# Five joints of a two-model block kernel: two weight blocks instead of one start on the unnormed x, with masks and reciprocal deviation in PSUM and one block's low halves on GpSimd

## The chip, the cores and the metric

The kernel runs on one core of a Trainium2 chip. The metric is the time of one execution on the device, in microseconds; the kernel before was timed three times, and the median counts. TensorE is called PE in the rows, VectorE DVE, ScalarE ACT, GpSimd POOL and SyncE SP.

## The reference, cut to what matters

Two models follow each other on one sequence of 256 tokens with 1024 features, all in float32. The first block is an adaptive RMS norm, a wide projection, a 31-tap convolution branch, a Mamba-2 scan, two output projections and a gated MLP. The second has a gated delta rule layer and a gated linear attention layer, each with an MLP of 4096 hidden features. What the change touches are the five places where a norm stands between two big matrix products:

```python
h = rms_norm(x, norm_ffn_w[i]) * (1.0 + scale) + shift          # joint "ffn"
x = x + gate * ffn_sublayer(h, w_ffn_in[i], w_ffn_down[i])
return rms_norm(x, final_norm_w)                                # joint "final"
...
m = _mixer_gdn(x, a_w_in[j], ...)        # qkv = silu(conv(x @ a_w_in)), decays exp(cumsum(g))
x = _layernorm(ALPHA * x + m, ln1_g[i], ln1_b[i])               # joints "ln1_0", "ln1_1"
x = _layernorm(ALPHA * x + relu(x @ w1) ** 2 @ w2, ln2_g[i], ln2_b[i])   # joint "ln2_0"
```

## The kernel before, in words

**Products.** x is kept feature-major: 8 tiles of 128 features by 256 tokens. A weight matrix comes in blocks of 1024 rows by 256 columns (1 MB), through a ring `raw` of four slots that SyncE fills in order. A block is two tiles (h = 0, 1) of 128 output features. To reach float32 accuracy each operand is split in a rounded high half and the rest: ScalarE copies `raw` to `whi` (L463, `split_hi`), VectorE or GpSimd subtracts to get `wlo` (L473, `split_lo`), both in rings of four tiles, that is, two blocks. TensorE then runs whi·HH + whi·HL + wlo·HH over 8 tiles of x (L596 to L598), 24 matmuls for a tile and 48 for a block, into one of four PSUM banks `acc`. A slot of `raw` is released by `split_lo`.

**Sections.** `split_section` walks a matrix on ScalarE, VectorE or GpSimd, `pe_section` on TensorE: after the splits for block b+1 come the results of block b, then `extra(b)`. Every engine works through its list in the order in which the program writes it; semaphores tie the lists together. The order is written by hand, there is no scheduler.

**Joints.** A norm needs all 8 tiles of the new x, which the last section before it (w_out, ffn_down, a_out, mlp2_0, b_out) produces two at a time with VectorE (L1957, L1961). So that TensorE isn't idle meanwhile, block 0 of the section behind a norm (ffn_in, a_qkv, mlp1_0, b_qk, mlp1_1) takes x unnormed: `act_first` makes squares SQX (L760) and the high half of gain times x, GHI (L761); `low_halves` makes GLO on VectorE (L794); `pe_early` multiplies block 0 with them, in between sums squares and x over features with matmuls against ones (L697 to L707: float32 operands, two records for each), and `scale_first` on VectorE repairs the product afterwards with mean and reciprocal deviation (L857 to L864). `norm_dve` meanwhile centres x (L934), scales it (L940), and makes the low half HL (L956) of the normed x; ScalarE makes the high half HH (L909). Block 1 (`pe_first`, L530 to L537) already needs HH, and HL right behind. `norm_pool` (L965, L967) writes the normed x back to X for the residual. Blocks 0 and 1 of the early section share their whi/wlo rings and PSUM banks with what is before them.

**a_qkv.** Each of its 12 blocks needs 8 operations of VectorE for a five-tap convolution (L1814) behind a copy by ScalarE (L1413); in blocks 3 to 10 VectorE also makes the decay matrices: six products of a 128x128 mask and a column (L2017 to L2021, `decay_sides`). The low halves of the weights are GpSimd's here. Behind the section TensorE reads the decay matrices (L2492).

ffn_in also carries four loads of 1 MB of adaptive-norm weights (`ADA_PLAN`) in the same ring `raw`, used up by VectorE (L1671).

## Time and profile before

| | us |
|---|---|
| median of 3 runs | 1563.12 (1562.01 to 1563.95) |
| the profiled execution | 1563.59 |
| its span, first to last instruction | 1561.9 |
| PE busy | 1428.2 (91%), 10981 matmul records |
| DVE busy | 1012.4 (65%) |
| ACT busy | 774.1 (50%) |
| POOL busy | 396.3 (25%) |
| chain that ended last, PE's share | 73% |
| chain that ended last, DVE's share | 13% |

Matmuls overlap, so a record lasts 284 ns while the next starts long before; what counts on TensorE is the distance from start to start. The joints lie at 452 us (ffn), 657 us (final), 963 us (ln1_0), 1162 us (ln2_0) and 1345 us (ln1_1).

### The profile page before, as it was taken

To read this page: it belongs to the slowest core of one execution; us is meant where nothing else is said; L and a number is where in the kernel's file an instruction comes from. 1 tells how busy PE (TensorE), PEld (TensorE's weight loads), DVE (VectorE), ACT (ScalarE), POOL (GpSimd) and SP (SyncE) were. 2 spreads that over 40 slices of the span, in tenths; PEclk is the share of its full clock that TensorE was granted. 3 is DMA by queue.
4 is the path that set the end of the run, shared out by engine and by line. 5 is a ranking of instruction groups with operands and counts; after the bars stand their busy time and mean duration, and the time that the engine had idled before them with its cause. 6 is when DMAs were issued, how large, how long until landed. Compare 5 with 4: busy or idle time off the path is not lost.

```text
span 1561.9 us, 27505 instructions
## 1 busy us (share of the span) xinstructions
PE 1428.2 (91%) x10981; PEld 1374.3 (88%) x10981; DVE 1012.4 (65%) x1739; ACT 774.1 (50%) x1211; POOL 396.3 (25%) x340
## 2 busy tenths in 40 slices
PE   4989999989898999898988889999999987999998
PEld 4989998988898999898878879999997976899997
DVE  5687868557676665669655557874465565876443
ACT  3434466574363433464573445664354634666333
POOL 1555774304300000157372400730005000200000
PEclk9899999999899999989999999999999999999999
DMA  9954553233746745625310005455553510365540
GB/s 355 365 163 133 165 162 109 82 108 121 238 155 218 226 157 162 208 81 162 109 55 1 1 1 162 139 186 181 178 167 97 178 39 10 127 189 184 174 155 28
DMA packets 202480, 223.74 MB, mean 143 GB/s; under 512 B 7608, under 2 KB 197723, under 8 KB 200317
## 3 DMA queue, kind: packets, MB, share of 16 engines
q1 hardware_dynamic: 201072, 220.67, 43.8%
q8 instruction: 80, 1.31, 0.4%
q10 hardware_dynamic: 1293, 1.47, 0.3%
q14 instruction: 35, 0.29, 0.1%
HBM read 221.07 MB, written 1.05 MB: 142 GB/s over the span
## 4 chain that ended last, share of the span: by engine, by line
PE 73%; DVE 13%; ACT 6%; issue 3%; DMA 2%; POOL 2%; SPq 0%; DVEq 0%; ACTq 0%; POOLq 0%
PE acc L596 18%; PE acc L598 17%; PE acc L597 17%; DVE GB L1814 2%; POOL H L967 1%; PE acc L530 1%; ACT whi L463 1%; PE acc L537 1%; DVE wlo L473 1%; PE acc L531 1%; DMA raw<-in_w_ffn_in 1%; DMA XIN<-in_x 1%; DVE SQX L940 1%; POOL AM L1185 1%; PE pm L2346 1%
## 5 line engine op out<-in xcount | busy, mean ns | idle before, releaser
L596 PE MATMUL acc<-HH,whi 128*128 128x256 f32 x1744 | 500.2, 287 | 26.3 <-issue 10.6
L463 ACT ACTIVATE whi<-raw 128x1024 fp32r<-128x1024 f32 (+2 forms) x380 | 378.8, 1029 | 241.3 <-PE acc L598 194.1
L597 PE MATMUL acc<-HL,whi 128*128 128x256 f32 x1744 | 495.1, 284 | 0.0
L598 PE MATMUL acc<-HH,wlo 128*128 128x256 f32 x1744 | 494.7, 284 | 0.0
L473 DVE TENSOR_TENSOR wlo<-raw,whi 128x1024 fp32r<-128x1024 f32 (+2 forms) x292 | 339.3, 1194 | 206.3 <-ACT whi L463 203.7
L596 PEld LDWEIGHTS acc<-HH,whi 128*128 128x128 f32 x1744 | 333.1, 191 | 34.0 <-issue 22.2
L597 PEld LDWEIGHTS acc<-HL,whi 128*128 128x128 f32 x1744 | 332.9, 191 | 0.3 <-issue 0.2
L598 PEld LDWEIGHTS acc<-HH,wlo 128*128 128x128 f32 x1744 | 332.8, 191 | 0.0
L473 POOL TENSOR_TENSOR wlo<-raw,whi 128x1024 fp32r<-128x1024 f32 x88 | 217.8, 2494 | 426.7 <-DVE wlo L473 272.1
L596 PE MATMUL acc<-HIDH,whi 128*128 128x256 f32 x688 | 195.7, 284 | 6.4 <-ACT whi L463 4.5
L598 PE MATMUL acc<-HIDH,wlo 128*128 128x256 f32 x688 | 195.4, 284 | 0.0
L597 PE MATMUL acc<-HIDL,whi 128*128 128x256 f32 x688 | 195.4, 284 | 0.0
L596 PEld LDWEIGHTS acc<-HIDH,whi 128*128 128x128 f32 x688 | 132.8, 193 | 7.0 <-issue 7.0
L597 PEld LDWEIGHTS acc<-HIDL,whi 128*128 128x128 f32 x688 | 132.8, 193 | 0.0
L598 PEld LDWEIGHTS acc<-HIDH,wlo 128*128 128x128 f32 x688 | 132.8, 193 | 0.0
L1800 DVE SCALAR_TENSOR_TENSOR pm<-UP,par,pm 128x256 f32<-128x256 f32 x158 | 66.9, 482 | 0.0
L530 PE MATMUL acc<-HH,whi 128*128 128x256 f32 x128 | 42.4, 351 | 15.6 <-ACT HH L909 6.7
L1552 ACT ACTIVATE TMP<-acc 128x256 f32<-128x256 f32 x60 | 23.1, 385 | 63.7 <-PE acc L598 58.9
L1185 POOL TENSOR_TENSOR AM<-ATT,gm 128x512 f32<-128x512 f32 x28 | 38.4, 1395 | 59.1 <-DVE ATT L2101 41.8
L2182 DVE TENSOR_TENSOR TMQ<-TMP 128x256 f32<-128x256 f32 x64 | 28.9, 452 | 37.4 <-ACT HIDH L1555 37.4
L1814 DVE SCALAR_TENSOR_TENSOR GB<-acc,par,GB 128x254 f32<-128x254 f32 (+1 forms) x96 | 45.1, 480 | 9.2 <-ACT GB L1413 6.4
L967 POOL TENSOR_SCALAR X<-SQX,par 128x256 f32<-128x256 f32 x8 | 8.2, 1036 | 159.4 <-DVE SQX L940 159.4
(542 smaller groups left out, 2531.1 us busy)
## 6 DMA issues: line engine op xcount, KB each, us to landing
raw<-in_mlp_w SPq DMA_DIRECT2D x64, 1024.0 KB, 5.3
raw<-in_w_in SPq DMA_DIRECT2D x36, 1024.0 KB, 5.3
raw<-in_w_ffn_in SPq DMA_DIRECT2D x22, 1024.0 KB, 5.3
raw<-in_a_w_in SPq DMA_DIRECT2D x16, 1024.0 KB, 5.7
raw<-in_b_w_in SPq DMA_DIRECT2D x12, 1024.0 KB, 5.3
raw<-in_w_ada_mix SPq DMA_DIRECT2D x8, 1024.0 KB, 5.6
ADR<-in_w_ada_ffn SPq DMA_DIRECT2D x8, 1024.0 KB, 11.1
...
```

The lines of the kernel that those rows point to most:

```text
L463: act.activation(whi[:, (s.t0 + 2 * u + h) % 4, 0:k], raw[:, place(s, b, u) % 4, 0:k, h * P:h * P + P], ACT.Copy).then_inc(hi_ready, 1)
L473: v.tensor_tensor(wlo[:, slot, 0:k], raw[:, place(s, b, u) % 4, 0:k, h * P:h * P + P], whi[:, slot, 0:k].bitcast(F32), ALU.subtract).then_ ...
L530: pe.matmul(acc[:, q, 0:T], whi[:, slot, i], hh, start=i == 0, stop=False)
L596: pe.matmul(acc[:, q, 0:T], whi[:, slot, i], hh, start=first and i == 0, stop=False)
L597: pe.matmul(acc[:, q, 0:T], whi[:, slot, i], hl, start=False, stop=False)
L598: m = pe.matmul(acc[:, q, 0:T], wlo[:, slot, i], hh, start=False, stop=final and i == k - 1)
L967: pool.tensor_scalar(dst[:, k], SQ[name][:, k], shift(k) if shift else 0.0, None, ALU.add)\
L1185: pool.tensor_tensor(AM[u][:, lv % 2].rearrange("p (s c) -> p s c", s=4), ATT[u][:], mask, ALU.mult).then_inc(am_ok, 1)
L1552: act.activation(TMP[:, q], acc[:, out_slot(s, u, h), 0:T], ACT.Relu, bias=evac_bias(s, b, u, h))\
L1800: c.tick(v.scalar_tensor_tensor(ACC[:, i] if w_ == CW - 1 else sum_, src, wt, sums.get(i, sum_), ALU.mult, ALU.add))
L1814: ins = v.scalar_tensor_tensor(d_, x_, pc(w, i + 24 * tap), d_, ALU.mult, ALU.add)
L2182: c.link(v.tensor_tensor(TMQ[:, q], TMP[:, q], TMP[:, q], ALU.mult))
```

## The change

It does seven things.

1. In the five early sections blocks 0 and 1 both take x unnormed (`pe_early` with four tiles; `scale_first` is called for block 0 ahead of HL and for block 1 behind it). Block 2 is the first that takes HH and HL.
2. The order inside the joint is new: one sum of squares and one of x, added up on VectorE, go to TensorE ahead of the last tile of the section before (`pe_parts`); the splits of block 1 are slipped between the steps (`mid`, `norm_dve`, `early_act`); the table load of ScalarE is moved ahead.
3. The reciprocal deviation is written to PSUM (`pm[:, 1, T:]`) for the scaling of x, and to NR for `scale_first`.
4. The low halves of block 2 go to GpSimd (`third`), and `norm_pool` of these joints waits until HL is complete. GpSimd starts with a_qkv's block 3 only then too; blocks 0 and 1 are VectorE's.
5. ffn_down and mlp2_0 are unrolled, and consecutive column pairs take turns in the four PSUM banks.
6. The decay masks are copied to PSUM once (`masks_in_psum`), and `decay_sides` reads them there; TensorE waits for `gm_l` too.
7. The four adaptive-norm loads of ffn_in come behind blocks 3, 5, 7, 9 instead of 1, 3, 5, 7; shifts and the gate logits of ln2_0 come one block later.

```diff
-                "ffn_in": (0, 1, 0, 1, 0, 1, 0, 1) + (0,) * 14}
+                "ffn_in": (0, 0, 0, 1, 0, 1, 0, 1, 0, 1) + (0,) * 12}
...
-            return (s.o0 + h) % 4
+            return (s.o0 + h + (2 * j if s.flat else 0)) % 4
...
+                    if s.name in NORM_BEFORE and last and h == 1:
+                        pe_parts(pe, NORM_BEFORE[s.name])
...
+        def pe_parts(pe, name):
+            mean = NORM[name][1]
+            pe.wait_ge(part_ok, PARTS[name] + (2 if mean else 1))
+            if mean:
+                pe.matmul(pm[:, 0, 0:T], ones, NR[:, 0] if is_long(name) else XP[:, 0], start=True, stop=False)
+            pe.matmul(pm[:, 1, 0:T], ones, SQX[:, 0], start=True, stop=False)
...
+            with_lo(first, range(6))
+            with_hi(first, whi, (6, 7))
+            with_hi(first, wlo, (6, 7))
+            with_lo(first, (6, 7)).then_inc(w_used, 1)
+            for tile in tiles[1:]:
+                open_(tile)
+                with_hi(tile, whi, range(8))
+                with_lo(tile, range(7))
+                pe.wait_ge(raw_used, 2 * s.w0 + tile[0] + 1)
+                with_hi(tile, wlo, range(8))
+                with_lo(tile, (7,)).then_inc(w_used, 1)
...
+                act.activation(pm[:, 1, T:], NR[:, 1], ACT.Exp, scale=-0.5).then_inc(n_std, 1)
+                act.activation(NR[:, 1], NR[:, 1], ACT.Exp, scale=-0.5)
                 for h in range(2):
-                    split_hi(act, SEC[EARLY[name]], 1, 1, h)
+                    split_hi(act, SEC[EARLY[name]], 2, 2, h)
...
-                v.scalar_tensor_tensor(sq[:, k], src[:, k], scale(k), NR[:, 1], ALU.mult, ALU.mult).then_inc(n_t, 1)
+                v.scalar_tensor_tensor(sq[:, k], src[:, k], scale(k), pm[:, 1, T:] if e else NR[:, 1], ALU.mult, ALU.mult)\
+                 .then_inc(n_t, 1)
...
+            if name in EARLY:
+                pool.wait_ge(n_hl, 8 * HN[name] + 8)
...
+            def third(name):
+                s = SEC[EARLY[name]]
+                pool.wait_ge(raw_used, 2 * (s.w0 + 2))
+                for h in range(2):
+                    split_lo(pool, s, 2, 2, h)
...
+            third("ffn")
+            third("final")
+            pool.wait_ge(n_hl, 8 * HN["final"] + 8)
...
-                    v.tensor_scalar(LF[:, 2 * h + tk], slo[:, 0:P], gcol(gd, 0, tk, h), None, ALU.mult)
+                    v.tensor_scalar(LF[:, 2 * h + tk], s_lo, gcol(gd, 0, tk, h), None, ALU.mult)
...
+            def masks_in_psum():
+                for i, m in enumerate((slo[:, 0:P], suo[:, 0:P], maskb[:, P:2 * P], maskf[:, 0:P])):
+                    c.tick(v.tensor_copy(pm[:, 3, i * P:i * P + P], m))
+                c.wait()
```

VectorE's list at the joint ln1_1, from the last two tiles of x on, before (L473 is a low half of weights, X<-X,acc the residual, L857 to L864 `scale_first`):

```order
L1957 TENSOR_TENSOR X<-X,acc 128x256 x2
L794 SCALAR_TENSOR_TENSOR GLO_ln_0_105<-X,par,GHI_ln_0_104 128x256 x4
L473 TENSOR_TENSOR wlo<-raw,whi 128x1024 x2
L928 TENSOR_SCALAR NR<-pm 128x256
L929 SCALAR_TENSOR_TENSOR NR<-pm,NR 128x256
L931 SCALAR_TENSOR_TENSOR NR<-pm,NR 128x256
L934 SCALAR_TENSOR_TENSOR X<-pm,X 128x256 x8
L940 SCALAR_TENSOR_TENSOR SQX<-X,par,NR 128x256 x8
```

And in the changed kernel, from the last tile of x to the repair of block 1:

```order
L2047 TENSOR_TENSOR X<-X,acc 128x256
L474 TENSOR_TENSOR wlo<-raw,whi 128x1024
L823 SCALAR_TENSOR_TENSOR GLO_ln_0_105<-X,par,GHI_ln_0_104 128x256
L990 TENSOR_SCALAR NR<-pm 128x256
L991 SCALAR_TENSOR_TENSOR NR<-pm,NR 128x256
L474 TENSOR_TENSOR wlo<-raw,whi 128x1024
L994 SCALAR_TENSOR_TENSOR NR<-pm,NR 128x256
L996 SCALAR_TENSOR_TENSOR X<-pm,X 128x256 x8
L1002 SCALAR_TENSOR_TENSOR SQX<-X,par,pm 128x256 x8
L902 COPY WB<-acc 128x2 x2
L1022 SCALAR_TENSOR_TENSOR HL<-SQX,par,HH 128x256 x8
```

The low half of block 1's second tile now stands between the mean and the variance, the scaling reads PSUM, and the repair (rows L902 to L916) stands once ahead of HL and once behind it. Two rows of the repair between L902 and L1022 are the ones of L857 to L864, for both tiles at once.

TensorE's list at the same joint in the changed kernel, from the first early matmul on (GHI and GLO are the halves of gain times x):

```order
L704 MATMUL acc<-GHI_ln_0_104,whi 128x258 x6
L724 MATMUL pm<-X,maskf 128x256 x2
L704 MATMUL acc<-GHI_ln_0_104,wlo 128x258 x6
L730 MATMUL pm<-SQX,maskf 128x256
L733 MATMUL pm<-SQX,maskf 128x256 x2
L711 MATMUL acc<-GLO_ln_0_105,whi 128x258 x6
```

Five sums against ones stand here where there were ten; two more stand ahead of the last tile of b_out, and the low half's six products now follow within the first tile.

VectorE's list in a_qkv, the decay sides of one head, before and in the changed kernel:

```order
L2017 TENSOR_SCALAR LF<-slo,gd 128x128
L2018 TENSOR_SCALAR LB<-suo,gd 128x128
L2017 TENSOR_SCALAR LF<-slo,gd 128x128
L2018 TENSOR_SCALAR LB<-suo,gd 128x128
L2020 TENSOR_SCALAR GM<-maskb,gd 128x128
L2021 TENSOR_SCALAR GM<-maskf,gd 128x128
```

```order
L2123 TENSOR_SCALAR LF<-pm,gd 128x128
L2124 TENSOR_SCALAR LB<-pm,gd 128x128
L2123 TENSOR_SCALAR LF<-pm,gd 128x128
L2124 TENSOR_SCALAR LB<-pm,gd 128x128
L2126 TENSOR_SCALAR GM<-pm,gd 128x128
L2127 TENSOR_SCALAR GM<-pm,gd 128x128
```

Nothing is moved here; the six operations read their mask from PSUM.

## Rows read from the trace of the kernel before

**Rows 1.** Windows: stretch; its us, busy time of PE, PEld, DVE, ACT, POOL; PEclk; DMA.

```profile
451.60:466.60 15.00, 14.98 (x108) 13.86 (x107) 12.97 (x29) 13.35 (x23) 0.00 (x0) 1.00 0.43 141
656.80:677.70 20.90, 16.04 (x102) 15.04 (x103) 16.40 (x32) 11.94 (x22) 8.16 (x4) 0.84 0.39 113
963.10:984.00 20.90, 19.33 (x118) 16.26 (x117) 18.66 (x44) 13.56 (x25) 4.96 (x8) 1.00 0.31 101
1161.90:1183.00 21.10, 18.21 (x110) 16.05 (x109) 18.16 (x42) 11.50 (x20) 9.48 (x20) 0.92 0.31 99
1345.10:1367.80 22.70, 19.44 (x118) 16.20 (x116) 20.44 (x46) 14.84 (x27) 8.16 (x8) 1.00 0.30 94
530.00:590.00 60.00, 60.00 (x507) 60.00 (x507) 35.93 (x55) 24.35 (x31) 0.00 (x0) 1.00 0.49 157
```

**Rows 2.** Timeline of PE at joint ln1_1: start us, us, what [idle before <-releaser].

```profile
1345.83 1.46 PE L697 MATMUL pm<-SQX,maskf 128*128 128x256 f32 x6
1347.13 1.46 PE L700 MATMUL pm<-XP,maskf 128*128 128x256 f32 x6
...
1367.84 0.36 PE L596 MATMUL acc<-HH,whi 128*128 128x256 f32 x1 [1.44 <-issue]
```

**Rows 3.** Groups of DVE in 1345 to 1368: xcount | busy us, mean ns.

```profile
L473 DVE TENSOR_TENSOR wlo<-raw,whi 128x1024 fp32r<-128x1024 f32 x4 | 4.7, 1221 | 1.8 <-ACT whi L463 1.8
L956 DVE SCALAR_TENSOR_TENSOR HL<-SQX,par,HH 128x256 fp32r<-128x256 f32 x8 | 3.9, 554 | 0.0
L940 DVE SCALAR_TENSOR_TENSOR SQX<-X,par,NR 128x256 f32<-128x256 f32 x8 | 3.8, 548 | 0.0
L934 DVE SCALAR_TENSOR_TENSOR X<-pm,X 128x256 f32<-128x256 f32 x8 | 2.7, 414 | 0.0
L859 DVE SCALAR_TENSOR_TENSOR acc<-NR,WB,acc 128x256 f32<-128x256 f32 x2 | 1.0, 490 | 0.1
...
L2182 DVE TENSOR_TENSOR TMQ<-TMP 128x256 f32<-128x256 f32 x2 | 0.8, 416 | 0.0
```

**Rows 4.** Waits of PE in 640 to 760: us in total, times, longest.

```profile
PE acc L596 <- DVE GB L1814: 5.3, 2, 3.7
PE acc L692 <- DVE X L1961: 4.9, 1, 4.9
PE pm L2492 <- DVE LB L2018: 2.1, 1, 2.1
PE acc L596 <- issue: 1.9, 2, 1.7
```

**Rows 5.** Windows at the joint final, columns as in rows 1.

```profile
661.00:668.00 7.00, 6.34 (x28) 5.83 (x29) 2.64 (x6) 5.59 (x9) 2.50 (x2) 0.58 0.25 89
...
681.00:688.00 7.00, 7.00 (x36) 7.00 (x37) 3.03 (x7) 1.08 (x2) 4.71 (x3) 0.55 0.66 166
```

**Rows 6.** Timeline of DVE before the joint final and in a_qkv.

```profile
652.50 6.73 DVE L794 SCALAR_TENSOR_TENSOR GLO_final<-X,par,GHI_final 128x256 fp32r<-128x256 f32 x6
...
721.11 0.28 DVE L2018 TENSOR_SCALAR LB<-suo,gd 128x128 f32<-128x128 f32 x1
...
723.84 2.39 DVE L2020 TENSOR_SCALAR GM<-maskb,gd 128x128 f32<-128x128 f32 x1
...
731.41 3.97 DVE L1814 SCALAR_TENSOR_TENSOR GB<-acc,par,GB 128x254 f32<-128x254 f32 x8
```

**Rows 7.** Timeline of POOL in a_qkv.

```profile
721.41 4.73 POOL L473 TENSOR_TENSOR wlo<-raw,whi 128x1024 fp32r<-128x1024 f32 x2 [0.32 <-ACT whi L463]
```

**Rows 8.** Timeline of DVE: the same kind of operation with its input in PSUM.

```profile
918.89 0.34 DVE L2137 TENSOR_SCALAR VNA<-acc,ab__690 128x128 f32<-128x128 f32 x1
919.15 0.34 DVE L2136 TENSOR_SCALAR VNA<-acc,ab__690 128x128 f32<-128x128 f32 x1
```

**Rows 9.** Waits of PE in 440 to 530, around the start of ffn_in.

```profile
PE acc L596 <- issue: 5.0, 4, 1.4
PE acc L596 <- ACT whi L463: 1.9, 3, 0.7
```

More of the change, by code:

```diff
@@ L488, in body @@
                 for h in range(2):
-                    if s.name in NORM_OF and eng is not nc.gpsimd and b == 0:
+                    if s.name in NORM_OF and b in (0, 2):
                         continue
-                    if split and not last:
+                    if split and s.name in NORM_OF and b == 1:
+                        if split is split_lo and h == 0:
+                            eng.wait_ge(raw_used, 2 * (s.w0 + 3))
+                        split(eng, s, 3, 3, h)
+                    elif split and not last:
                         split(eng, s, b + 1, u + 1, h)
@@ L497, in body @@
                         evac(b, u, h, j)
+                        if mid and last and h == 0:
+                            mid()
                 if extra:
@@ L633, in program @@
         XC0 = {"conv": 0, "ln1_0": 8, "ln2_0": 17, "ln1_1": 26, "ln2_1": 35}
-        PARTS = {"ffn": 0, "final": 1, "ln1_0": 2, "ln2_0": 4, "ln1_1": 6}
+        PARTS = {"ffn": 0, "final": 2, "ln1_0": 3, "ln2_0": 6, "ln1_1": 8}
         RANK = {name: i for i, name in enumerate(EARLY)}
@@ L681, in pe_early, with with_hi, with_lo, open_ @@
             o0 = SEC[BEFORE[name]].o0 + 4
-            place_ = [(h, (s.t0 + h) % 4, out_slot(s, 0, h)) for h in range(2)]
-            for h in range(2):
-                pe.wait_ge(hi_ready, s.t0 + h + 1)
-                pe.wait_ge(raw_used, 2 * s.w0 + h + 1)
-            late = 2 if SEC[BEFORE[name]].chunks > 1 else 0
-            pe.wait_ge(acc_free, s.o0 + late + 1)
-            def with_hi(h, slot, q, ks):
+            tiles = [(2 * b + h, (s.t0 + 2 * b + h) % 4, out_slot(s, b, h)) for b in range(2) for h in range(2)]
+            def with_hi(tile, weights, ks):
+                i, slot, q = tile
                 for k in ks:
                     pe.wait_ge(g_hi, g + k + 1)
-                    pe.matmul(acc[:, q, 0:w], whi[:, slot, k], hi[:, k, 0:w], start=k == 0, stop=False)
-            with_hi(*place_[0], range(6))
-            px, ps = parts(name)
-            pe.wait_ge(part_ok, PARTS[name] + (2 if mean else 1))
-            for i, t_ in enumerate(ps):
-                pe.matmul(pm[:, 1, 0:T], ones, t_, start=i == 0, stop=False)
+                    pe.matmul(acc[:, q, 0:w], weights[:, slot, k], hi[:, k, 0:w],
+                              start=k == 0 and weights is whi, stop=False)
+            def with_lo(tile, ks):
+                i, slot, q = tile
+                for k in ks:
+                    pe.wait_ge(g_lo, g + k + 1)
+                    m = pe.matmul(acc[:, q, 0:w], whi[:, slot, k], lo[:, k, 0:w], start=False, stop=k == 7)
+                return m
+            def open_(tile):
+                i = tile[0]
+                pe.wait_ge(hi_ready, s.t0 + i + 1)
+                pe.wait_ge(acc_free, s.o0 + i + 1)
+            first = tiles[0]
+            open_(first)
+            with_hi(first, whi, range(6))
             if mean:
-                for i, t_ in enumerate(px):
-                    pe.matmul(pm[:, 0, 0:T], ones, t_, start=i == 0, stop=False)
                 for k in (6, 7):
@@ L704, in pe_early @@
                 m.then_inc(n_mean, 1)
+            pe.wait_ge(raw_used, 2 * s.w0 + 1)
+            with_hi(first, wlo, range(6))
+            if not is_long(name):
+                pe.wait_ge(part_ok, PARTS[name] + (3 if mean else 2))
+                pe.matmul(pm[:, 1, 0:T], ones, SQX[:, 4], start=False, stop=False)
             for k in (6, 7):
@@ new lines, in more, with mid @@
+                if b == last - 1 and name in ("ffn", "final"):
+                    v.wait_ge(raw_used, 2 * e.w0)
+                    for h in range(2):
+                        split_lo(v, e, 0, 0, h)
+            def mid():
+                if not is_long(name):
+                    v.wait_ge(n_sq, 8 * n + 6)
+                    v.tensor_tensor(SQX[:, 4], SQX[:, 4], SQX[:, 5], ALU.add).then_inc(part_ok, 1)
+                low_halves(v, c, name, (6,))
+            return dict(extra=more, mid=mid)
@@ L1169, in _ @@
             pool.nop().then_inc(mask2, 1)
-            lo_section(SEC["a_qkv"])
+            third("ffn")
+            third("final")
+            pool.wait_ge(n_hl, 8 * HN["final"] + 8)
+            s = SEC["a_qkv"]
+            for b in range(3, s.nb):
+                for h in range(2):
+                    split_lo(pool, s, b, b % 4, h)
+            for h in range(2):
+                split_lo(pool, SEC["a_z"], 0, 0, h)
             lo_section(SEC["a_z"])
@@ L1186, in _ @@
                                            ALU.mult).then_inc(am_ok, 1)
+            third("ln1_0")
             norm_pool(pool, "ln1_0", par_col("ln1_b"), X)
@@ L1206, in _ @@
                     sums_to(W05[:, lv // 2, d, lv % 2 * P:lv % 2 * P + P], lv, d)
+            third("ln2_0")
             pool.wait_ge(n_t, 8 * NORM["ln2_0"][0] + 1)
@@ L1219, in _ @@
             pool_shift(pool, "ln2_0")
+            third("ln1_1")
             norm_pool(pool, "ln1_1", par_col("ln1_b", 8), X)
```

282 lines of the change are left out of this document (158 added, 124 removed).

## The prediction

> **What bounds the kernel now.** The first view to read is the chain that ended last: TensorE has 73% of it, VectorE 13%. So the question is where TensorE isn't fed. The second is a quiet stretch: between 530 and 590 us TensorE starts 507 matmuls in 60 us, at a granted clock of 1.00 [rows 1]. With a few records missing I use 0.119 us from start to start, so a block of 48 costs 5.71 us. A sum against ones costs more: three of them (six records) fill the 1.30 us from 1345.83 to 1347.13 [rows 2], 0.43 us each. With these two prices every joint can be billed. A joint's own work is 96 matmuls, 11.4 us, and its sums [all rows 1]:
>
> - ffn: 15.0 us, own 11.4 + 5 x 0.43 = 13.6, lost 1.4.
> - final: 20.9 us, own 11.4 + 3 x 0.43 = 12.7, lost 8.2; the 4.9 us wait for VectorE's X [rows 4] is in it.
> - ln1_0: 20.9 us, own 11.4 + 10 x 0.43 = 15.7, lost 5.2; ln1_1 likewise 22.7 - 15.7 = 7.0.
> - ln2_0: 21.1 us, own 11.4 + 6 x 0.43 = 14.0, lost 7.1.
>
> The joints lose 29 us. A third view, the waits of TensorE in a_qkv, adds 5.3 + 2.1 + 1.9 = 9.3 us [rows 4]. In ffn_in another 6.9 us go in seven waits, three of them for ScalarE's high half, that is, for weights that came late [rows 9].
>
> **What sets the wait in a joint.** VectorE's list. At ln1_1 it is busy 20.4 of 22.7 us [rows 1], and block 2 starts only at 1367.84, 1.44 us after TensorE was through with block 1 [rows 2]; VectorE's low half of block 2 is the last thing it needs. With two blocks early, TensorE has 5.7 us more to do before it asks for HH, and that covers the waits for HH and HL. What is late next must be asked of VectorE's list again, since block 3's low half stands behind everything.
>
> **ln1_1 and ln1_0.** TensorE first. The two sums moved ahead of the last tile are only moved, but they wait for VectorE: behind the sixth tile of x come a square and GHI on ScalarE, then a GLO and four additions, some 4.1 us at 0.42 to 0.49 each, against TensorE's tile of 2.9 us. So 1.2 us are waited there, and with the sums themselves (0.9) the first early matmul comes 2.1 us later than now. Then 96 matmuls and five sums, 13.6 us, and block 2, 5.7: TensorE could start block 3 at 21.4 us behind today's first early matmul, or at 23.3 in ln1_0, with its shift of 16 matmuls in between. Now VectorE, whose last tile of x is there 0.95 us behind the first early matmul: low half 1.2, GLO 0.5, mean 0.86, low half 1.2, variance 0.43, centring 2.7, scaling 2.7 (from PSUM: I take L934's price, the same form with one input in PSUM, not L940's 3.8), repair 2.1 (2 x (0.15 + 0.49 + 0.43)), HL 3.4 (8 x 0.42, L2182's price for two inputs in SBUF, since GpSimd's X now waits; L956's 3.9 beside GpSimd is the other end), repair 2.1, TMQ and HIDL of block 0 1.7, low half of block 3 1.2 [rows 3]. That is 20.1; with 2.1 and 0.95 it ends at 23.2, and 0.9 later because GpSimd's X runs beside its last part. So block 3 starts at 24.1. Today it starts at 22.7 + 5.7 = 28.4 (ln1_0: 28.5, with its shift). Gain 4.3 each; block 4's low half then comes 0.3 late: **4.0 each, 8.0 together**. GpSimd's two low halves of block 2, 2.4 us each [rows 7], start when ScalarE has split it and end some 3 us ahead of TensorE's need. Bounds: 2 each if VectorE's last part pays double for two-input operations, 5.2 if the parts aren't waited for.
>
> **ln2_0.** The same list, but the sums are ready long before, and VectorE is through with block 3's low half at 21.8 us, ahead of TensorE, which does shift and gate logits first. New is a wait: the logits need all of X, which GpSimd writes only behind HL now. HL is done at 17.5 us, eight operations at ln1_0's 0.62 us (4.96 for 8, rows 1) take 5.0, and TensorE asks at 0.9 + 13.1 + 5.7 + 1.9 = 21.6: 0.9 late. Behind GpSimd's X stand its masks W67 and the shift of X, which nobody needs before b_v is done. **7.1 - 0.9 = 6.2 us**; bounds 3 (ln1_1's 1.02 us each, rows 1) and 7.1.
>
> **ffn.** One sum less, 0.4. Block 2 waits 0.5 for ScalarE (table load and gate of block 0 stand behind HH), the parts 0.3, hops and HL 0.5: 1.3 lost instead of 1.4, and the first of the seven waits, 1.0 us before block 3, is covered. **1.5 us**, bounds 0 and 2.5. The four adaptive-norm loads sit in the same ring two blocks later with the same pattern (a slot is freed by VectorE behind block b, reloaded, and split for block b+3). I count the other 5.9 us [rows 9] as moved, not saved; bounds -1 and +3.
>
> **final and a_qkv.** (1) VectorE was late with X because six GLO took 6.7 us while GpSimd split a_qkv's block 0 [rows 6]; alone they would take 6 x 0.42 = 2.5. GpSimd is silent there now, and the banks take turns, so the wait of 4.9 goes, but for 0.6 for the last square. (2) Behind that wait the granted clock was 0.58 over 7 us [rows 5], that is, 1.2 GHz for most of them; without the wait I take it as 2.4 GHz. With the rest of the loss, (1) and (2) give 8.2 - 0.6 = 7.6. (3) The waits in a_qkv. A mask product takes VectorE 0.28 us alone, but 2.4 when GpSimd is in a low half, and it ends (723.84 + 2.39) when GpSimd's pair ends (721.41 + 4.73) [rows 6, 7]. The convolution, with an input in PSUM, keeps its 3.97 us for eight. With the masks in PSUM each product takes 0.26 from start to start [rows 8], six 1.6: VectorE's need for a block becomes 3.9 + 1.6 = 5.5 us, just below TensorE's 5.71. TensorE keeps 1.4 before block 4 (ScalarE's exponential behind VectorE's gates, then ScalarE's and GpSimd's halves) and 0.9 before block 5: 9.3 - 2.3 = 7.0. Together **14.6 us**. The second low stretch, 0.55 at 681 to 688 [rows 5], began behind small products of 32 columns, and these stay: its 3.2 us (0.45 x 7) stay. The four copies of masks cost 1.0 by the PSUM price, 2.4 more if one meets a GpSimd operation; VectorE is 3 us ahead of block 5 there. The added wait on `gm_l` costs two mask products, 0.5, behind b = 10, ahead of block 11's end.
>
> The rows say that a mask in SBUF waits for GpSimd and an input in PSUM doesn't. The Trainium skill's page "SBUF — State Buffer", section "Who interferes with whom", states a lock behind it: outside the two-port modes an operation of VectorE with at most one SBUF input doesn't contend. The same section speaks against `third`: an operation with two SBUF inputs contends with a GpSimd operation that reads SBUF. By it HL and the additions beside `third` would wait, which is rival B.
>
> **The rivals.** (B) VectorE's list is longer than billed: `third` and GpSimd's X slow its two-input operations as at 652 us (1.12 each instead of 0.42) [rows 6]. Then the ln1 joints and ffn give nothing: 1532.8 + 9.5 = 1542. For it: busy 20.4 of 22.7 us. Against: `third` lies beside centring and scaling, which have an input in PSUM. (C) PSUM doesn't free VectorE, the change doesn't do what it says: the GB and LB waits stay (7.0), and each of four joints pays a GpSimd low half of 2.4: 1532.8 + 16.6 = 1549. Against: the 3.97. (D) The parts are there in time (3 x 1.2) and the clock doesn't fall at 681 (3.2): 1526. (E) Slower: the clock falls in the early stretch of the joints, as it did behind the wait of 4.9. TensorE waits 1.2 us for the parts, and again for squares; if each joint then runs its 96 early matmuls at 1.2 GHz, that costs 11.4 us each, 57 in all: 1590. It decides from three joints on. Against: ln1_1's window shows 1.00 despite a wait of 1.44 [rows 1, 2].
>
> **How the numbers follow.** 1.5 + 14.6 + 8.0 + 6.2 = 30.3. The profiled execution took 1563.6 (span 1561.9 and 1.7 around it), 0.5 above the median: 1563.6 - 30.3 = 1533.3, against the median 1532.8. Chances: this case (1528 to 1537) 0.55, B 0.20, D 0.14, C 0.08, E 0.03. The range 1522 to 1545 takes in B and D with their bounds and leaves out C and E. A difference under 0.2% (3 us) can't be told from none: faster 0.95, same 0.02, slower 0.03.
>
> **What would show it.** Scaling of x at 2.7 us for eight; mask products all at 0.26 from start to start; no wait of TensorE for GB over 1 us in a_qkv behind block 5; the first block with HH starting without a wait; block 3 of mlp1 waiting for VectorE's low half; no low clock around 661. Wrong would be: waits for the parts over 2 us, GpSimd's low half as releaser of block 2, a granted clock under 0.9 in a joint, or more than 7 us of waits in ffn_in.

## The result, and the profile after

The changed kernel took 1519.61 us (median of 4 runs, 1518.09 to 1522.63) against 1562.57 for the kernel before: ratio 0.974, 95% interval 0.972 to 0.976. That is 43 us faster, where 30.3 were forecast, and 2.4 us below the range. Run once more beside the kernel before it took 1521.69 (6 runs, 1517.78 to 1528.29), ratio 0.977 (0.974 to 0.980), so 36 to 43 us is what the change gives. The profiled execution of the first set is its slowest, 1522.63, with a span of 1520.9 against 1561.9: 41.0 us between the two traces, and these are accounted for below. A wait is given as the rows print it, as TensorE's idle time, or, where starts are compared, from start to start less the 0.12 us that a matmul takes anyway, which is some 0.16 us more.

The windows from a joint's first early matmul to its last [before: rows 1], in the order ffn, final, ln1_0, ln2_0, ln1_1 (us, busy of PE, PEld, DVE, ACT, POOL, PEclk, DMA):

```profile
451.60:465.40 13.80, 13.27 (x104) 12.55 (x102) 11.95 (x27) 10.83 (x21) 4.82 (x2) 1.00 0.58 182
653.90:666.60 12.70, 12.54 (x102) 12.09 (x101) 9.00 (x19) 9.77 (x21) 4.80 (x2) 1.00 0.67 176
940.90:954.60 13.70, 13.70 (x108) 13.44 (x107) 13.53 (x34) 9.43 (x20) 4.77 (x2) 1.00 0.52 162
1131.30:1146.40 15.10, 13.49 (x107) 13.07 (x105) 14.56 (x36) 8.79 (x19) 5.96 (x4) 1.00 0.41 125
1308.70:1322.30 13.60, 13.60 (x108) 13.34 (x107) 13.43 (x34) 9.37 (x20) 4.77 (x2) 1.00 0.53 160
```

At both ln1 joints TensorE is busy all the time, and the clock is 1.00 in all five. TensorE's timeline at ln1_1 [before: rows 2] and at ln2_0 shows what is left: a wait for the part of x, none ahead of the first block with HH (1322.36), one ahead of block 3, and in ln2_0 one ahead of the first block with HH:

```profile
1304.88 0.70 PE L691 MATMUL pm<-XP,maskf 128*128 128x256 f32 x2 [1.07 <-DVE SQX L882]
...
1322.36 0.28 PE L537 MATMUL acc<-HH,whi 128*128 128x256 f32 x1
...
1329.31 0.35 PE L606 MATMUL acc<-HH,whi 128*128 128x256 f32 x1 [1.08 <-issue]
```

```profile
1146.47 0.36 PE L537 MATMUL acc<-HH,whi 128*128 128x256 f32 x1 [1.68 <-ACT QK L1660]
```

What ScalarE does ahead of that QK (the copy of block 0 out of its bank), with the repair's last operation on the bank's first tile by VectorE and the zeroing of the gate weights' tile `gw` by GpSimd:

```profile
1143.07 0.94 POOL L1295 MEMSET gw<- 33x1024 f32 x1
1143.40 0.49 DVE L914 TENSOR_SCALAR acc<-acc,WB 128x256 f32<-128x256 f32 x1
1144.46 0.32 ACTq L1655 DMA_DIRECT2D gw<-in_b_gate_w  x1
...
1145.48 0.30 ACTq L1656 DMA_DIRECT2D gw<-in_b_gate_b  x1
1145.83 0.66 ACT L1660 ACTIVATE QK<-acc 128x256 f32<-128x256 f32 x2 [2.48 <-issue]
```

VectorE's groups in 1308 to 1331 [before: rows 3] (xcount | busy us, mean ns):

```profile
L474 DVE TENSOR_TENSOR wlo<-raw,whi 128x1024 fp32r<-128x1024 f32 x4 | 4.8, 1216 | 0.0
L1022 DVE SCALAR_TENSOR_TENSOR HL<-SQX,par,HH 128x256 fp32r<-128x256 f32 x8 | 3.2, 480 | 0.0
L1002 DVE SCALAR_TENSOR_TENSOR SQX<-X,par,pm 128x256 f32<-128x256 f32 x8 | 3.2, 476 | 0.0
L996 DVE SCALAR_TENSOR_TENSOR X<-pm,X 128x256 f32<-128x256 f32 x8 | 2.7, 415 | 0.0
```

TensorE's waits in 632 to 740, the joint final and a_qkv [before: rows 4]:

```profile
PE acc L606 <- issue: 1.4, 2, 1.0
PE pm L733 <- ACT SQX L786: 0.2, 1, 0.2
```

The mask products, with their input in PSUM, take 0.26 us from start to start in a_qkv too, under GpSimd's low halves [before: rows 6]:

```profile
693.33 0.34 DVE L2124 TENSOR_SCALAR LB<-pm,gd 128x128 f32<-128x128 f32 x1
693.59 0.34 DVE L2126 TENSOR_SCALAR GM<-pm,gd 128x128 f32<-128x128 f32 x1
693.85 0.34 DVE L2127 TENSOR_SCALAR GM<-pm,gd 128x128 f32<-128x128 f32 x1
```

**Where the 41.0 us went.** Like instructions of both traces are set side by side: the difference of their starts grows or shrinks where time is won or lost. The clock's part is (1 - granted clock) summed over windows of 1 us; it comes in pieces of 1.7 us.

| stretch | forecast | found | of it clock |
|---|---|---|---|
| up to the joint ffn | 0 | 0.8 | |
| ffn, ffn_in, start of ffn_down | 1.5 | 2.3 | 0 |
| final and a_qkv | 14.6 (2.9 of it clock) | 21.3 | 8.5 |
| ln1_0 | 4.0 | 5.1 | 0 |
| start of mlp2_0 | 0 | 1.9 | 1.7 |
| ln2_0 | 6.2 | 5.6 | 0 |
| gated linear attention | 0 | 1.5 | 1.7 |
| ln1_1 | 4.0 | 5.5 | 0 |
| start of mlp2_1 | 0 | -1.5 | -1.7 |
| last norm | 0 | -1.4 | -1.7 |
| sum | 30.3 | 41.1 | 8.5 |

Some 32.6 us are shorter waits, where 27.4 were forecast, and 8.5 are clock, where 2.9 were: of the miss of 10.8, 5.6 are clock and 5.2 are waits, these spread over many places with no more than 1.5 in one. (The rows are rounded; the traces differ by 41.0.) The kernel before also paid it behind each of VectorE's waits in a_qkv, at 728, 755 and 772, three stretches that the prediction didn't bill (before; in front of the third stands a wait of 1.2 us, at 771.8, which all kernels here have):

```profile
728.30:732.30 4.00, 3.78 (x20) 3.81 (x21) 3.86 (x13) 1.89 (x3) 0.14 (x1) 0.57 0.67 225
755.00:759.00 4.00, 3.99 (x21) 3.99 (x22) 3.79 (x10) 0.00 (x0) 0.00 (x0) 0.58 0.80 260
772.50:776.50 4.00, 4.00 (x6) 1.52 (x5) 0.00 (x0) 1.37 (x3) 0.00 (x0) 0.57 0.73 237
```

The same work in the changed kernel, 17 to 24 us earlier (from 711, 734 and 749 us), runs at 1.00; only the stretch that the prediction kept, behind the products of 32 columns, is there. The window from 699 is for comparison with masks_sbuf below:

```profile
669.50:676.50 7.00, 7.00 (x36) 7.00 (x36) 6.58 (x17) 2.64 (x3) 4.73 (x2) 0.51 0.03 10
699.00:706.00 7.00, 7.00 (x61) 7.00 (x61) 6.73 (x19) 3.55 (x6) 5.89 (x3) 1.00 0.87 272
734.00:741.00 7.00, 7.00 (x65) 7.00 (x65) 4.00 (x9) 4.48 (x7) 1.40 (x1) 1.00 0.55 182
749.00:756.00 7.00, 6.92 (x37) 5.04 (x38) 0.34 (x4) 5.01 (x6) 0.00 (x0) 1.00 0.47 152
```

### The profile page after: what moved, and what is told of

It is laid out like the page before. It is cut to its first block, busy times and chain, and to the rows that moved or that the text cites. A ratio compares the mean times of both kernels' runs of the same rounds, so it can differ in the third digit from the quotient of the medians.

```text
span 1520.9 us, 27248 instructions
## 1 busy us (share of the span) xinstructions
PE 1404.4 (92%) x10967; PEld 1360.6 (89%) x10967; DVE 999.6 (66%) x1777; ACT 772.5 (51%) x1216; POOL 407.2 (27%) x344
## 4 chain that ended last, share of the span: by engine, by line
PE 78%; DVE 8%; ACT 6%; issue 3%; POOL 3%; DMA 2%; SPq 0%; ACTq 0%; DVEq 0%; POOLq 0%
PE acc L606 18%; PE acc L608 18%; PE acc L607 18%; PE acc L704 2%; PE acc L537 2%; POOL H L1037 1%; PE acc L538 1%; PE acc L544 1%; ACT whi L464 1%; DMA raw<-in_w_ffn_in 1%; DVE wlo L474 1%; DMA XIN<-in_x 1%; PE acc L711 1%; POOL AM L1270 1%; PE pm L2455 1%
## 5 line engine op out<-in xcount | busy, mean ns | idle before, releaser
L464 ACT ACTIVATE whi<-raw 128x1024 fp32r<-128x1024 f32 (+2 forms) x380 | 379.7, 1030 | 244.5 <-PE acc L608 193.5
L606 PE MATMUL acc<-HH,whi 128*128 128x256 f32 x1664 | 477.0, 287 | 18.7 <-issue 7.6
L608 PE MATMUL acc<-HH,wlo 128*128 128x256 f32 x1664 | 471.4, 283 | 0.0
L607 PE MATMUL acc<-HL,whi 128*128 128x256 f32 x1664 | 471.0, 283 | 0.0
L474 DVE TENSOR_TENSOR wlo<-raw,whi 128x1024 fp32r<-128x1024 f32 (+2 forms) x288 | 335.3, 1195 | 189.3 <-ACT whi L464 187.3
L474 POOL TENSOR_TENSOR wlo<-raw,whi 128x1024 fp32r<-128x1024 f32 x92 | 226.5, 2480 | 745.8 <-ACT whi L464 709.0
L606 PEld LDWEIGHTS acc<-HH,whi 128*128 128x128 f32 x1664 | 316.6, 190 | 25.3 <-issue 12.7
L607 PEld LDWEIGHTS acc<-HL,whi 128*128 128x128 f32 x1664 | 316.9, 190 | 0.3 <-issue 0.2
L608 PEld LDWEIGHTS acc<-HH,wlo 128*128 128x128 f32 x1664 | 316.3, 190 | 0.0
L537 PE MATMUL acc<-HH,whi 128*128 128x256 f32 x128 | 39.1, 332 | 12.2 <-ACT HH L1582 5.2
L606 PE MATMUL acc<-YH,whi 128*128 128x256 f32 x128 | 38.5, 301 | 5.9 <-DVE H L1985 3.4
```

The lines of the kernel that those rows point to most:

```text
L464: act.activation(whi[:, (s.t0 + 2 * u + h) % 4, 0:k], raw[:, place(s, b, u) % 4, 0:k, h * P:h * P + P], ACT.Copy).then_inc(hi_ready, 1)
L474: v.tensor_tensor(wlo[:, slot, 0:k], raw[:, place(s, b, u) % 4, 0:k, h * P:h * P + P], whi[:, slot, 0:k].bitcast(F32), ALU.subtract).then_ ...
L537: pe.matmul(acc[:, q, 0:T], whi[:, slot, i], hh, start=i == 0, stop=False)
L606: pe.matmul(acc[:, q, 0:T], whi[:, slot, i], hh, start=first and i == 0, stop=False)
L607: pe.matmul(acc[:, q, 0:T], whi[:, slot, i], hl, start=False, stop=False)
L608: m = pe.matmul(acc[:, q, 0:T], wlo[:, slot, i], hh, start=False, stop=final and i == k - 1)
```

## The experiments

No run takes the second early block back alone, so the 16 us of the three joints ln1_0, ln2_0 and ln1_1 are read from the aligned traces and not divided between that block and the new order. All but before_masks_psum and before_again start from the changed kernel. Each was timed beside the kernel before; its median is given, and where it matters the ratio. "Loss" is the clock's part in its trace from 440 us to TensorE's last matmul: 27.3 in the kernel before, 18.7 in the changed one. It is more than the time lost where the clock is low while TensorE waits anyway.

**Does the clock belong to the waits in a_qkv?** masks_sbuf:

```diff
-                s_lo, s_uo, m_b, m_f = (pm[:, 3, i * P:i * P + P] for i in range(4))
+                s_lo, s_uo, m_b, m_f = slo[:, 0:P], suo[:, 0:P], maskb[:, P:2 * P], maskf[:, 0:P]
```

> The changed kernel, but the six mask products of a head read their masks from SBUF again; the copies to PSUM stay. Theory A (the waits for VectorE in a_qkv bring the low clock with them): the waits of the kernel before come back, 10.0 us of stalls from start to start against 1.7 now (+8.3), and behind them TensorE runs at 1.2 GHz in stretches that aren't in the changed kernel's trace between 690 and 760, 5 us as in the kernel before: 1519.6 + 13 = 1533. Theory B (the low stretches of the kernel before fell there by chance): only the waits come back, no stretch under 0.9 of the clock between 690 and 760, 1519.6 + 8 = 1528.

Measured 1532.94 us, ratio 0.983 (0.980 to 0.986), 13 us behind the changed kernel. Its waits of TensorE in 632 to 765, its mask products beside GpSimd, and windows behind the waits:

```profile
PE acc L606 <- DVE GB L1904: 3.6, 1, 3.6
PE pm L2603 <- DVE GM L2127: 2.7, 1, 2.7
```

```profile
690.70 2.44 DVE L2124 TENSOR_SCALAR LB<-suo,gd 128x128 f32<-128x128 f32 x1
693.06 2.43 DVE L2123 TENSOR_SCALAR LF<-slo,gd 128x128 f32<-128x128 f32 x1
```

```profile
699.00:705.00 6.00, 4.71 (x22) 4.75 (x23) 5.71 (x17) 2.52 (x3) 1.08 (x1) 0.50 0.59 171
739.70:743.70 4.00, 3.97 (x21) 4.00 (x22) 3.56 (x8) 0.14 (x1) 0.00 (x0) 0.57 0.76 261
756.50:760.50 4.00, 4.00 (x6) 1.70 (x7) 0.22 (x3) 1.15 (x2) 0.00 (x0) 0.57 0.84 262
```

The alignment with the changed kernel's trace gives 12.3 us between 676 and 776 us alone, 6.6 of them in the two waits and 5.7 in matmuls at the low clock behind them and behind the wait of 1.2 at 756. That is theory A in its places and its time, with less wait than it said (6.6 for 8.3) and a little more clock.

before_masks_psum is the kernel before with this step alone:

```diff
+                for i, m in enumerate((slo[:, 0:P], suo[:, 0:P], maskb[:, P:2 * P], maskf[:, 0:P])):
+                    c.tick(v.tensor_copy(pm[:, 3, i * P:i * P + P], m))
+                c.wait()
...
-                    v.tensor_scalar(LF[:, 2 * h + tk], slo[:, 0:P], gcol(gd, 0, tk, h), None, ALU.mult)
+                    v.tensor_scalar(LF[:, 2 * h + tk], pm[:, 3, 0:P], gcol(gd, 0, tk, h), None, ALU.mult)
```

> The kernel before with this one part of the change alone: masks copied to PSUM, products read them there, TensorE waits for the last pair too. Theory A (waits bring the low clock): the waits for GB and LB, 7 to 8 us, go, and with them the stretches at 729, 756 and 773 (1.4 + 1.7 + 1.7 by their windows): 1562.6 - 12.5 = 1550. Theory B (clock by chance): 1562.6 - 7.5 = 1555, stretches of low clock still there behind 715. The joint final keeps its wait of 4.9 in both.

Measured 1552.92 (7 runs, 1549.28 to 1557.14) beside 1561.09, ratio 0.996 (0.994 to 0.998): 6 to 8 us by the times, theory B's number. The trace says otherwise: 12.9 us less between 677 and 780 us, the waits for GB gone, the last wait 1.0 instead of 2.1, the stretches at 681, 729 and 755 not there, the one at 773 left. But the stretch at 681 (3.1 of the 12.9) lies ahead of the first mask product, at 706, so this edit can't have taken it away. The masks' part is 9.8: 6.6 of waits and 3.2 of clock, of which theory A had 4.8. The next run shows how much such stretches vary.

before_again, the kernel before:

> The kernel before once more, for the places of its low-clock stretches. The prediction billed 2.9 us of clock to the change, the first pair of traces shows 8.5 between 640 and 790 us alone: five stretches (11.9 us) in the kernel before, one double one (3.4) in the changed one. Theory A (the clock falls behind the waits of 3.9 and 2.1 in a_qkv in most executions): at least three stretches between 640 and 790 again, 27 +- 3 us lost behind 440. Theory B (the first trace was unlucky): two at most there, under 22 us in all.

Measured 1559.78 (12 runs, 1555.39 to 1563.10). Its trace has four stretches between 640 and 790 us, 10.2 us, and loses 28.8 in all: theory A. But the same code crosses 677 to 780 us 3.6 us quicker than in the first trace, 1.5 of it because one stretch fewer falls there (its wait of 2.2 at 744 has no low clock behind it), 2.1 because VectorE's GB is waited for once (3.7) instead of twice (1.6 and 3.7). So neither the stretches nor the waits of the kernel before are quite the same each time, and its first trace was on the dear side. Over all fourteen traces: with the masks in SBUF (before, before_again, masks_sbuf) 11.9, 10.2 and 8.5 us are lost between 640 and 790; with the masks in PSUM 5.1 in before_masks_psum, which keeps the wait of 4.9 ahead of final, and 0 to 3.4 in the ten others. That puts the change's clock gain there at about 8 us (11.0 in the mean of the two traces of before, 2.7 in the mean of the ten).

By place, not all of it hangs on the waits. Behind the wait of 4.9 the clock fell in all three traces that have it. The three traces with the masks in SBUF have six waits of over 2 us for GB or for the masks; behind five of them it fell, and with the masks in PSUM no trace but delay24's (next) has such a stretch there. This link is shown. The stretch at 773, behind the wait of 1.2 us, comes in all three, but also in five of the eleven with the masks in PSUM (before_masks_psum, no_turns, nr_sbuf, nr_sbuf_third_dve, pool_x_early), and the one that starts in the products of 32 columns (681 before, 669.6 after) is missing in three of the eleven (before_masks_psum, after_again, third_dve): these two come and go without the masks.

**A wait made on purpose.** delay24:

```diff
                     decay_sides(b - 3)
+                    if b == 6:
+                        for i in range(24):
+                            t_ = (LF, LB, GM)[i // 8]
+                            c.tick(v.tensor_scalar(t_[:, 8 + i % 8], pm[:, 3, 0:P], gcol(gd, 0, 0, 3), None, ALU.mult))
+                        c.wait()
```

> The changed kernel with 24 more mask products (0.26 us each, 6.2 in all, their results aren't used) on VectorE at one place, behind block 6 of a_qkv. VectorE is 2 to 2.5 us ahead of TensorE there, so TensorE waits some 4 us once. Theory A (a wait of that size brings the low clock): a stretch of about 3.4 to 7 us at 1.2 GHz behind the wait, 1.5 to 3.2 us more: 1519.6 + 4 + 2.3 = 1526. Theory B (clock by chance): the wait alone, 1519.6 + 4 = 1523.6, and a granted clock of 1.00 behind it.

Measured 1533.74 (1528.62 to 1537.26), and neither number held. At the place itself theory A did: TensorE waits 1.8 us, less than I took, as VectorE was further ahead, and another 1.0 at the end of the section, and behind the first wait the clock is low:

```profile
718.00:722.00 4.00, 4.00 (x23) 4.00 (x23) 3.86 (x12) 2.33 (x3) 0.58 (x1) 0.57 0.90 250
```

Together 4.7 us up to 776 us. The other 8 lie where the code is the same in both kernels, nearly all of it clock (loss 26.0 against 18.7). All four executions took 1528.6 or more, longer than any of the ten of the changed kernel (1528.3 at most), so chance from one execution to the next doesn't explain them well; why a wait here should cost clock hundreds of microseconds later is open.

**Is it the turns of the banks?** no_turns:

```diff
-            return (s.o0 + h + (2 * j if s.flat else 0)) % 4
+            return (s.o0 + h) % 4
...
-                            pe.wait_ge(acc_free, 2 * j + s.o0 + h + (1 if s.flat else 3))
+                            pe.wait_ge(acc_free, 2 * j + s.o0 + h + 3)
...
-                pe.wait_ge(acc_free, s.o0 + i + 1)
+                pe.wait_ge(acc_free, s.o0 + i + (3 if is_long(name) and i < 2 else 1))
```

> The changed kernel, but the column pairs of ffn_down and mlp2_0 all use the same two banks again (the sections stay unrolled), so that the first early tile waits for VectorE's last additions. Theory A (the six slow GLO beside GpSimd made the wait of 4.9, and they are fast now): about 1 us of wait at each of the two joints and half a microsecond at each of three column changes, +3 to +4: 1523. Theory B (it is the banks that took the wait away): 4.9 of wait at the joint final, a low clock behind it worth 2.9, and as much again at ln2_0: 1519.6 + 8 to 15 = 1528 to 1535.

Measured 1527.66 (1521.30 to 1529.09). In its trace no wait of TensorE stands at final (632 to 680) and none at ln2_0 beside the known 1.68; up to 1030 us it is level with the changed kernel. The 7.6 us that it loses behind that are clock in stretches that only its trace has (loss 25.8), as this one, behind the wait at mlp2_0 for HIDL (the low half of the MLP's hidden tiles, HIDH is the high one), which both kernels have; no_turns, then the changed kernel:

```profile
1037.00:1041.00 4.00, 4.00 (x21) 4.00 (x22) 2.35 (x2) 0.81 (x1) 0.00 (x0) 0.57 0.42 119
```

```profile
1038.30:1042.30 4.00, 4.00 (x33) 4.00 (x34) 2.36 (x2) 1.68 (x2) 0.00 (x0) 1.00 0.43 141
```

So the turns are worth about half a microsecond without the clock, and they are not what took the wait of 4.9 away. What is left is GLO, which GpSimd no longer slows: 1.01 us each at the joint final before, 0.48 in both kernels here; no run slows it again. Theory A's direction, smaller than it said.

**How much of that is chance?** after_again, the changed kernel:

> The changed kernel itself once more, beside the kernel before. In the six traces so far TensorE's waits stand at the same places with the same lengths, but the low-clock stretches behind them come or stay away: the first trace of the changed kernel loses 18.7 us to them behind 440 us, its two close relatives no_turns and delay24 25.8 and 26.0. Theory A (chance from execution to execution): other stretches appear this time, the loss is anywhere from 17 to 27 us, and the median lies at 1519 to 1527. Theory B (the change fixes the pattern): the same eight stretches and 1519.6 within 1.5 us.

Median 1521.69. Nearly every wait stands at the same place with the same length as in the first trace (2.00 at mlp2_0, 2.39 at mlp2_1, 1.85 at ln2_0; ahead of blocks 4 and 5 of a_qkv 1.3 and 0.45 stand for 0.55 and 1.20), but the loss is 21.0, with eleven stretches instead of eight, and none at all between 640 and 790: the loss of 3.4 us that the prediction kept is not always there either. Theory A, but the stretches aren't drawn one by one. Behind ln2_0 the traces of after_again, no_turns, delay24 and hid_late have the same five, at the same distances from each other, 10.2 us in all, where the first trace of the changed kernel loses 5.1. What decides between such patterns is open.

**What is PSUM worth to the scaling of x?** nr_sbuf (the signal to VectorE moves with the value that it reads):

```diff
-                act.activation(pm[:, 1, T:], NR[:, 1], ACT.Exp, scale=-0.5).then_inc(n_std, 1)
-                act.activation(NR[:, 1], NR[:, 1], ACT.Exp, scale=-0.5)
+                act.activation(pm[:, 1, T:], NR[:, 1], ACT.Exp, scale=-0.5)
+                act.activation(NR[:, 1], NR[:, 1], ACT.Exp, scale=-0.5).then_inc(n_std, 1)
...
-                v.scalar_tensor_tensor(sq[:, k], src[:, k], scale(k), pm[:, 1, T:] if e else NR[:, 1], ALU.mult, ALU.mult)\
+                v.scalar_tensor_tensor(sq[:, k], src[:, k], scale(k), NR[:, 1], ALU.mult, ALU.mult)\
```

> The changed kernel, but the scaling of x reads the reciprocal deviation from SBUF. Theory A (the input in PSUM is what makes the scaling shorter): the eight operations take 3.8 us as in the kernel before instead of 3.2 now, and another 0.3 at the start; +0.9 at ln1_1, where TensorE waits for VectorE, 0.1 at ln1_0, nothing elsewhere: +1 without the clock, 1521. Theory B (two inputs in SBUF beside GpSimd's low halves cost far more, 1.12 each as with GLO in the kernel before): the eight take 6 to 9 us and block 2's product waits for HL too: +3 to +5 at each ln1 joint, 1528.

Measured 1541.11 (1536.24 to 1543.77), ratio 0.989: 20 us slower than the changed kernel, the largest effect of a single edit here. VectorE's scaling at ln1_1 and GpSimd's timeline there:

```profile
L1002 DVE SCALAR_TENSOR_TENSOR SQX<-X,par,NR 128x256 f32<-128x256 f32 x8 | 7.5, 999 | 0.0
```

```profile
1329.22 4.95 POOL L474 TENSOR_TENSOR wlo<-raw,whi 128x1024 fp32r<-128x1024 f32 x2 [150.56 <-ACT whi L464]
```

TensorE then waits ahead of the first block with HH (3.3 instead of 0 at either ln1 joint, 4.2 instead of 1.8 at ln2_0, 2.1 instead of 0.7 at ffn), because that block's bank is free only behind the repair of block 0. Some 10 us are waits, the rest is clock (loss 28.7). Theory B's mechanism: the eight take 7.5 us, the joints wait 3.3 each, and the clock, which it didn't bill, makes it dearer than it said.

nr_sbuf_third_dve adds third_dve's edit (next), so that GpSimd is silent beside the scaling:

> Both undone at once: the scaling of x reads the reciprocal deviation from SBUF, and the low halves of block 2 are VectorE's, so that GpSimd is silent beside the scaling. nr_sbuf alone cost 19 us, its eight operations taking 7.5 us beside GpSimd's low half instead of 3.2. Theory A (two inputs in SBUF are slow only beside GpSimd's operations): the eight take 3.7 us, and the kernel stands 1 us behind third_dve: 1528. Theory B (two inputs in SBUF are slow by themselves after the table work of ScalarE, or NR is late): 7.5 us again, 1540.

Measured 1527.19 (1520.97 to 1533.38). The eight operations, in 1300 to 1330 us:

```profile
L1002 DVE SCALAR_TENSOR_TENSOR SQX<-X,par,NR 128x256 f32<-128x256 f32 x8 | 3.2, 484 | 0.0
```

Theory A: the same 3.2 us as from PSUM (484 ns each against 476). For this operation an input in PSUM makes nothing quicker; it only keeps it out of GpSimd's way. The section "Who interferes with whom" of the Trainium skill's page "SBUF — State Buffer" has it so: a VectorE instruction with two SBUF inputs contends with a GpSimd instruction that reads SBUF, one with at most one SBUF input doesn't, outside the two-port modes. The trace agrees for two inputs (999 ns each beside GpSimd, 484 without). The mask products have one SBUF input and did wait, 2.4 us, so the condition on the modes matters; no row here shows the mode of an operation. By that rule `third` was a danger, and it would have been one but for the deviation in PSUM.

**The third block's low halves.** third_dve:

```diff
-            third("ffn")
-            third("final")
...
-            third("ln1_0")
...
-            third("ln2_0")
...
-            third("ln1_1")
...
             if e:
+                for h in range(2):
+                    split_lo(v, e, 2, 2, h)
                 v.wait_ge(n_hh, 8 * HN[name] + 1)
```

> The changed kernel with the low halves of block 2 on VectorE, behind the scaling of x, instead of on GpSimd. Theory A (VectorE's list sets the start of block 3, as the prediction has it): 2.4 us more in every joint's list; at ln1_1 TensorE already waits 1.2 us for it (+2.4), at ln1_0 it is 0.8 ahead (+1.6), ln2_0, ffn and final have slack or up to 1 us: +4 to +6 without the clock, 1525. Theory B (VectorE is no longer on the path in the joints): under 1 us without the clock, 1520.

Measured 1528.33 (1521.36 to 1529.57). Waits ahead of the first block with HH of 1.3 at both ln1 joints, 2.06 instead of 1.24 ahead of block 3 at ln1_1, and 1.5 for X at ln2_0; ffn gains 0.6. Joint by joint the aligned traces give, without the clock, +1.9 at ln1_0, +1.8 at ln2_0, +1.9 at ln1_1 and -0.6 at ffn, 4.9 us: theory A's 4 to 6. Only part of it stands ahead of block 3, where the theory had it.

**GpSimd's X beside HL.** pool_x_early:

```diff
-            if name in EARLY:
-                pool.wait_ge(n_hl, 8 * HN[name] + 8)
```

> The changed kernel, but GpSimd writes the normed x as soon as the scaled x is there, beside VectorE's HL, without waiting for it. Theory A (GpSimd slows VectorE's operations with two inputs in SBUF): HL at 0.55 each instead of 0.41, as in the kernel before (+1.2), and block 3 1.2 to 2 us later at ln1_1, 0.4 to 1 at ln1_0: +2 to +3 without the clock, 1522. Theory B (no contention of weight): no wait grows, the residual x is there earlier, 1519.6.

Measured 1525.26 (1523.22 to 1526.78). HL at ln1_1, and what TensorE waits ahead of block 3:

```profile
L1022 DVE SCALAR_TENSOR_TENSOR HL<-SQX,par,HH 128x256 fp32r<-128x256 f32 x8 | 4.2, 596 | 0.0
```

```profile
PE acc L606 <- issue: 1.9, 1, 1.9
```

Theory A in kind: 0.8 more there and 0.7 at ln1_0, 1.5 instead of 2 to 3. The rest of the median, 2 us over after_again's and 4 over the first one's, I can't place.

**A version that beats both.** The changed kernel's trace still had waits of 1.7, 2.0 and 2.4 us at the starts of ffn_down, mlp2_0 and mlp2_1. hid_late:

```diff
-                pe.wait_ge(hid_lo, 32 * k + 32 + 4)
+                pe.wait_ge(hid_lo, 32 * k + 24 + 4)
...
+                if s.name in all_hid() and u == 3:
+                    pe.wait_ge(*all_hid()[s.name])
...
-            if s.name not in NORM_OF:
+            if s.name not in NORM_OF and s.name != "mlp2_0":
                 pe.wait_ge(acc_free, s.o0 + 4)
...
+                if b == 19:
+                    v.nop().then_inc(hid_ok, 1)
```

> The changed kernel with one more step: ffn_down, mlp2_0 and mlp2_1 wait for the last eight (four) hidden tiles only at the last quarter of the first column pair, which is the first that reads them, and mlp2_0 not for all four banks. In the changed kernel's trace TensorE waits 1.7, 2.0 and 2.4 us at these three starts (releasers VectorE's HIDL and ScalarE's high half). Theory A (these waits are for the last hidden tiles): 1.2, 1.9 and 1 to 2.3 go, and the low clock behind two of them now and then: 1519.6 - 5 = 1515. Theory B (the weights' high halves, named as releaser at mlp2_1, hold it): 2 us at most, 1518.

Measured 1513.36 (1507.93 to 1519.54), ratio 0.971 (0.967 to 0.975): 8 us better than after_again; the aligned traces place 0.7, 2.1 and 2.7 of them at the three starts, 1.5 of the last being a low stretch behind the wait that isn't there now: theory A. Left are waits of 0.8 at ffn_down, nothing at mlp2_0 and 1.1 at mlp2_1.

both adds the other edit, with the sums and results that use these loads moved back to later blocks:

```diff
-                "ffn_in": (0, 0, 0, 1, 0, 1, 0, 1, 0, 1) + (0,) * 12}
+                "ffn_in": (0, 0, 0, 1, 0, 0, 0, 1, 0, 0, 0, 1, 0, 0, 0, 1) + (0,) * 6}
```

> hid_late with the four adaptive-norm loads of ffn_in behind blocks 3, 7, 11 and 15 instead of 3, 5, 7 and 9. In the changed kernel TensorE loses 1.6 + 0.7 + 1.6 + 0.8 + 1.9 = 6.6 us behind the last three of them, nothing behind the first. Theory A (a load costs only because the ring hasn't recovered from the one before): with four blocks between them 3 to 6 us less than hid_late, 1511. Theory B (each load costs its 2.3 us wherever it stands once the joint's lead is used up): no difference to hid_late, 1515.

Measured 1505.80 (6 runs, 1499.11 to 1507.58), ratio 0.965 (0.962 to 0.967), the fastest here, 14 to 16 us ahead of the changed kernel. TensorE's waits in 440 to 600 are these, with none for weights in ffn_in:

```profile
PE acc L611 <- DVE TMQ L2075: 0.8, 1, 0.8
PE acc L537 <- ACT TMP L1496: 0.6, 1, 0.6
```

Theory A to the full: all 6.6 us went. Here a load in the ring of four costs 2.3 us when it comes two blocks behind the one before, and nothing when it comes four blocks behind.

## Why the prediction was wrong, point by point

The direction held, and so did the mechanisms but for the wait named at ln2_0; the size didn't. The sum is 10.8 us short of the traces, 5.6 in the clock and 5.2 in many small waits.

- **The clock, term (2) and "the second low stretch stays".** This is the step that failed. The price of a wait was taken as the wait alone, but for the one of 4.9. The rows for 728, 755 and 772 us were in the trace; they stand right behind waits of 3.9, 2.2 and 1.4 (from start to start). Billed like the 4.9, they would have added 5.1 and brought the forecast to 1527.7. That is inside the range but still 6 to 8 us above the measured medians; the rest is in the waits below. And the 3.2 us "kept" are there in some executions only. masks_sbuf shows the link for the first two (3.4 us), and all three traces with the masks in SBUF have it. The third (1.7) hangs on a wait that the change doesn't touch and comes in five of eleven traces with the masks in PSUM too: that the changed kernel's first trace lacks it is in part luck.
- **The waits of a_qkv, term (3).** 7.0 forecast, 8.3 found (10.0 from start to start before, 1.7 now). The products take 0.26 as forecast; what was kept ahead of blocks 4 and 5 (2.3) measured 0.55 and 1.20. Terms (1) and (2) gave 8.0 at the joint against 7.6.
- **ln1_0, ln1_1.** 5.1 and 5.5 instead of 4.0. The waits for the parts are 1.13 and 1.23 (forecast 1.2). VectorE's low half of block 3 ends 22.5 us behind the old first early matmul at ln1_1, not at 24.1: half a microsecond because its last tile came sooner, 0.9 because GpSimd's X, which now runs beside the last part only, slowed nothing of weight. Scaling measured 3.2, not the 2.7 I took from the form with X as output: an input in PSUM isn't quicker by itself (nr_sbuf_third_dve). HL took 3.2 for 3.4.
- **ln2_0.** 5.6 for 6.2, but not by the wait named. X was there in time. TensorE waited 1.7 us ahead of block 2 for its bank, which ScalarE's QK frees behind VectorE's repair of block 0. I never asked which bank hangs on that. Nor was the repair the last thing missing: it was through with the bank's first tile at 1143.9. ScalarE's list has four loads of gate weights ahead of QK; they wait for GpSimd's zeroing of `gw`, which now stands behind `third`, and kept ScalarE until 1145.8. By these times QK could have ended at 1144.3, ahead of TensorE's need at 1144.8, an estimate that no run tests.
- **ffn.** 2.3 for 1.5. 1.4 at the joint, 0.4 in ffn_in, where 6.6 us of waits stay as forecast, and 0.4 at the start of ffn_down, which I didn't look at.
- **The rivals.** B did not come: HL took 3.2 us and no more. Its mechanism is real, as nr_sbuf shows, and the deviation in PSUM is what kept it away from the scaling. That nr_sbuf lands at 1541, beside B's 1542, is luck: B counts 9.5 us from 1532.8, the run has some 10 of waits and 10 of clock on 1519.6. C is refuted by 0.26 for each product and by before_masks_psum's trace. E is refuted by five windows at 1.00. D had the right idea, that more clock could come back, and the wrong share: the parts weren't in time, and the stretch that it let go, at 681, was still there in the first trace.
- **The range.** Its low end left out a sum in which several small terms all come out on the good side, and gave the clock no range of its own, though it changes from one execution to the next, which the prediction's one trace couldn't show. Waits (32) and clock (8 in the mean) make 40 us, 1522.6; the first comparison lies 3 us on the good side of that, the repetition 4 on the other.
